# Float32 layers on one core: the parts of p as an interleaved or scattered moving operand, and one gate tile in matmuls of 256 columns

## What is computed

```python
def hybrid_layer(h, p_l, pos, w_in, w_out, g_pre, g_post, g_hg, lb_f, lb_b, w_pg, w_pp, g_ple):
    u = rmsnorm(h, g_pre)
    z = u @ w_in                                   # (512, 2048) @ (2048, 9216)
    ...
    y_hg = o_hg * jax.nn.silu(hg.astype(f32))
    ...
    gate = jax.nn.sigmoid((h @ w_pg).astype(f32))
    e = (p_l @ w_pp).astype(f32)                   # (512, 256) @ (256, 2048)
    h = h + rmsnorm((gate * e).astype(h.dtype), g_ple)
    return h
```

## Time and profile before

| | |
|---|---|
| median of three runs | 3124.75 us |
| span of the profiled execution, first to last instruction | 3121.8 us |
| TensorE matmuls busy | 3041.7 us, 97% |
| TensorE weight loads busy | 2410.3 us, 77% |
| VectorE, ScalarE, GpSimd busy | 53%, 39%, 42% |
| mean granted TensorE clock | 0.992 |

### The profile page before, as it was taken

How to read it: one execution, slowest core, us unless ns; L and a number is a source line. 1 busy time by engine, 2 the same in 40 slices (tenths; PEclk the granted TensorE clock), 3 DMA queues, 4 the chain that set the end, 5 groups by cost and what they waited for, 6 DMA issues and landing times.

```text
span 3121.8 us, 44761 instructions
## 1 busy us (share of the span) xinstructions
PE 3041.7 (97%) x15518; PEld 2410.3 (77%) x15518; DVE 1641.8 (53%) x2261; ACT 1227.8 (39%) x2164; POOL 1316.8 (42%) x1006
## 2 busy tenths in 40 slices
PE   8999999999999999999999999999999999999997
PEld 6877778777777787777777777788777777777886
DVE  5377666554554414657565664461275646645412
ACT  6445444333334333444233333453332333334532
POOL 4444344333334244452434344444534434443444
PEclk9999999999999999999999999999999999999998
DMA  6222212222222323233322222233342222222322
GB/s 240 103 84 98 81 69 82 79 73 76 74 74 81 122 94 135 95 109 121 128 71 97 76 81 84 79 114 129 108 160 90 85 88 81 85 81 81 145 98 94
DMA packets 60872, 307.70 MB, mean 99 GB/s; under 512 B 5712, under 2 KB 6096, under 8 KB 29520
## 3 DMA queue, kind: packets, MB, share of 16 engines
q1 hardware_dynamic: 38224, 259.54, 23.2%
q10 hardware_dynamic: 22528, 46.60, 4.3%
HBM read 287.77 MB, written 18.35 MB: 98 GB/s over the span
## 4 chain that ended last, share of the span: by engine, by line
PE 48%; issue 27%; POOL 14%; DVE 7%; DVEq 2%; ACT 1%; POOLq 0%; DMA 0%; ACTq 0%; SPq 0%
PE z L302 37%; POOL w_low L239 13%; DVE work L1428 2%; DVEq L1510 1%; DVE work L1417 1%; PE z L318 1%; PE turned L302 1%; PE scores L526 1%; PE scores L499 1%; PE o_bank L506 1%; DVE work L1579 1%; PE scores L302 1%; PE scores L536 1%; PE o_bank L546 1%; PE v_bank L335 1%
## 5 line engine op out<-in xcount | busy, mean ns | idle before, releaser
L239 POOL TENSOR_TENSOR w_low<-w_raw,w_high 128x512 fp32r<-128x512 f32 x932 | 1256.0, 1352 | 1785.0 <-ACT w_high L688 1778.3
L302 PE MATMUL z<-u_high,w_high 128*128 128x512 f32 x3408 | 1371.7, 402 | 2.9 <-POOL w_low L239 2.2
L302 PE MATMUL z<-u_high,w_low 128*128 128x512 f32 x3408 | 1329.0, 390 | 0.0
L302 PE MATMUL z<-u_low,w_high 128*128 128x512 f32 x3408 | 1327.7, 390 | 0.0
L688 ACT ACTIVATE w_high<-w_raw 128x512 fp32r<-128x512 f32 x928 | 578.5, 629 | 1275.1 <-PE z L302 1177.4
L302 PEld LDWEIGHTS z<-u_high,w_high 128*128 128x128 f32 x3408 | 640.1, 188 | 149.2 <-issue 16.9
L302 PEld LDWEIGHTS z<-u_low,w_high 128*128 128x128 f32 x3408 | 640.3, 188 | 143.7 <-issue 14.4
L302 PEld LDWEIGHTS z<-u_high,w_low 128*128 128x128 f32 x3408 | 639.6, 188 | 136.1
L1579 DVE TENSOR_TENSOR work<-work 128x512 f32<-128x512 f32 x87 | 99.7, 1146 | 363.8 <-ACT work L935 350.6
L1241 DVE TENSOR_TENSOR work<-z,work 128x512 f32<-128x512 f32 x110 | 76.1, 692 | 166.1 <-PE z L302 145.1
L1269 DVE SCALAR_TENSOR_TENSOR work<-z,work 128x512 f32<-128x512 f32 x56 | 38.7, 692 | 188.9 <-PE z L302 188.3
(11 more groups left out here) (265 smaller groups left out, 3106.9 us busy)
## 6 DMA issues: line engine op xcount, KB each, us to landing
w_raw<-in_wt SPq DMA_DIRECT2D x241, 1024.0 KB, 4.8
out_hT<-work ACTq DMA_DIRECT2D x8, 1024.0 KB, 7.6
work<-out_hT ACTq DMA_DIRECT2D x8, 1024.0 KB, 10.3
work<-in_xT SPq DMA_DIRECT2D x4, 1024.0 KB, 17.9
e_scratch<-work ACTq DMA_DIRECT2D x1, 4096.0 KB, 19.5
work<-in_xT ACTq DMA_DIRECT2D x4, 1024.0 KB, 10.5
work<-in_gw ACTq DMA_DIRECT2D x2, 1792.0 KB, 10.0
work<-in_dec ACTq DMA_DIRECT2D x12, 256.0 KB, 2.6
```

Of the source, the lines that this page charges most:

```text
L239: pool.tensor_tensor(WL[:, 4 * q:4 * q + 4, :], RAW[:, t.odd, 512 * q:512 * q + 512].rearrange("p (k c) -> p k c", k=4), WH[:, 4 * q:4 * q ...
L302: mm = pe.matmul(bank[:], w[:, k, :], u[:, k, :], start=(k == 0 and n == 0), stop=(k == KT - 1 and n == 2))
```

## The change

It has two parts. First, the parts of p are laid out differently in the same four rows of u_low. For k = 0 the high and the low part lie interleaved in rows 12 and 13: element t of the high part at 2t, of the low part at 2t + 1. For k = 1 each part has a row of its own, in another order: token 4a + b lies at 128b + a, so four consecutive tokens are 128 elements apart. The writers (ScalarE's copy and VectorE's subtraction) write in that order, and the matmuls read in token order, so that the bank's columns come out as before. Second, the matmuls of the second gate tile are issued in two halves of 256 columns each, every one with its weight load. `skip_group_check` is a flag of the program's checks and gives no instruction.

```diff
+WHOLE = (slice(0, 512),)
+HALVES = (slice(0, 256), slice(256, 512))
...
-        PH, PL = UL[:, 12:14, :], UL[:, 14:16, :]
+        both = UL[:, 12:14, :].rearrange("p a t -> p (a t)").rearrange("p (t a) -> p t a", a=2)
+        spread = [UL[:, r, :].rearrange("p (b a) -> p a b", b=4) for r in (14, 15)]
+        PH, PL = [both[:, :, 0], spread[0]], [both[:, :, 1], spread[1]]
+
+        def p_order(k, ap):
+
+            return ap.rearrange("p (a b) -> p a b", b=4) if k else ap
...
+            def gate_quarter(t, q, order, gen=None, spare=None, behind=2):
...
+                    for n, (w, u) in enumerate(((WH, UH), (WH, UL), (WL, UH))):
+                        for c in order:
+                            mm = pe.matmul(bank[:, c], w[:, k, :], u[:, k, c], start=(k == 0 and n == 0 and c is order[0]),
+                                           stop=(k == KT - 1 and n == 2), skip_group_check=len(order) > 1)
+                mm.then_inc(sem("w_free"), 1)
...
-                        mm = pe.matmul(Z[m % 2][:], w[:, 2 * n + k, :], u[:, k, :], start=(k == 0 and i == 0),
+                        mm = pe.matmul(p_order(k, Z[m % 2][:]), w[:, 2 * n + k, :], u[k], start=(k == 0 and i == 0),
                                        stop=(k == 1 and i == 2))
...
-                    quarter(Tile(T_HGG + m), q, 0 if m == 0 else None, SPARE.get(m), 4 if m in (4, 5) else 2)
+                    gate_quarter(Tile(T_HGG + m), q, HALVES if m == 1 else WHOLE, 0 if m == 0 else None, SPARE.get(m),
+                                 4 if m in (4, 5) else 2)
...
             for k in range(2):
-                copy(PH[:, k, :], MIX[:, 14 + k, :], "ph_ready")
+                copy(PH[k], p_order(k, MIX[:, 14 + k, :]), "ph_ready")
...
             for k in range(2):
                 v.wait_ge(sem("ph_ready"), k + 1)
-                v.tensor_tensor(PL[:, k, :], MIX[:, 14 + k, :], PH[:, k, :].bitcast(F32),
+                v.tensor_tensor(PL[k], p_order(k, MIX[:, 14 + k, :]), PH[k].bitcast(F32),
                                 ALU.subtract).then_inc(sem("p_split"), 1)
```

More of the change, by code:

```diff
@@ L303, in quarter @@
                                        stop=(k == KT - 1 and n == 2))
+                mm.then_inc(sem("w_free"), 1)
+            def gate_quarter(t, q, order, gen=None, spare=None, behind=2):
+                bank = Z[t.odd] if spare is None else spare
+                if q == 0 and spare is None:
+                    if t.c in (T_HGG, T_HGG + 1):
+                        pe.wait_ge(sem("e_out"), 16)
+                    else:
+                        pe.wait_ge(sem("z_free"), t.times(1, 1 - T_HGG - behind))
+                pe.wait_ge(sem("l_ready"), t.times(4, q + 1))
+                for k in range(4 * q, 4 * q + 4):
+                    if gen is not None:
+                        pe.wait_ge(sem("u_ready"), gen * 16 + k + 1)
+                    for n, (w, u) in enumerate(((WH, UH), (WH, UL), (WL, UH))):
+                        for c in order:
+                            mm = pe.matmul(bank[:, c], w[:, k, :], u[:, k, c], start=(k == 0 and n == 0 and c is order[0]),
+                                           stop=(k == KT - 1 and n == 2), skip_group_check=len(order) > 1)
                 mm.then_inc(sem("w_free"), 1)
```

## The result

The changed kernel takes 3133.77 us (median of five runs, 3133.41 to 3134.44) where the kernel before takes 3124.11 in the runs beside it (five runs, 3123.7 to 3125.0): ratio 1.0032, 95% interval 1.002 to 1.0044, so 9.66 us slower. The forecast was +6.4; the sign was right, the size was not, and the time lies just above the range. The profiled execution took 3133.56 us with a span of 3131.8, 10.0 more than before.

The account below looks back on a forecast made before the run. TensorE's matmuls, filling 97% of the span, were taken as the bound, with slack at two places. Longer reads 9.6 less 3.3 swallowed, +0.1 start, +0 halves gave +6.4 on 3124.75: 3131.2 us, range 3124.3 to 3133.5.

Parts of the forecast that it names:

- Part 1: p's product, 48 matmuls of k = 0 reading every second element: 0 us extra, half rate kept as a rival.
- rival C: p's product: k = 0 at half rate as well as k = 1, +15.9 us, 3140.7 us; chance 0.09.
- Part 2: p's product, scattered reads of k = 1: half rate, +0.213 us for each of 45 matmuls, 9.6 us.
- Part 3: p's product: TensorE's stalls behind late x and weight transfers vanish, swallowing 3.3 of 9.6 us and leaving +6.3 us.
- Part 4: Start of p's product: ScalarE's scattered write of k = 1 delays TensorE by +0.1 us, bounds 0 and +0.6.
- Part 5: Second gate tile as 96 half-width matmuls: -0.3 to +0.6 us, hidden by the third tile's 1.6 us stall, so 0.
- B: p's product: scattered reads are hidden, steps stay 0.227 us, only ScalarE's later start remains, 3124.9 us; chance 0.26.
- A: The forecast itself, p's product: k = 1 at half rate, k = 0 free, 3130.5 to 3132.5 us; chance 0.50.

Follow-up runs that it names:

- The third set of patterns: Kernel before, with chosen read patterns (repeats, alignments) in the 16 banks of p's product and second gate tile in varied widths; steps 0.216 to 0.459 us, no whole time given.

## Why the prediction was wrong, and where it was right

**Part 1, "I take 0 and keep half rate as a rival": the step that failed.** The interleaved read cost 0.220 us a matmul, 9.9 us in all. Row and rule both misled me. VectorE's every second element for nothing says nothing about TensorE's moving operand, for VectorE takes 1.3 ns for each of them (0.679 us / 512) where TensorE takes 0.44 (0.2267 us / 512); I had called it the nearest row and used it as if it were near. And the Trainium skill (Advanced Engine Details and Errata, SBUF Cachelines) asks for two hits on a 16-byte line: I counted an element as a hit, so that every second element had two. The third set of patterns shows that for this stream a hit is an access of two elements. Counted so, the rule holds in all the patterns of the table and gives k = 0 its half rate. It would still have been wrong on k = 1, which has one access on a line at a time and would be at half rate too, as in rival C.

**Part 2, half rate for k = 1, +0.213 a matmul: mis-sized.** It measured +0.057, or +0.045 alone. The sum has a slip as well: it takes the 0.427 against 0.213, though the kernel's own step is 0.2267, and 0.200 x 45 would be 9.0 instead of 9.6. The upper half of the range was never near. The reason given, that the surplus of a steady step shows a stream at the limit of its read rate, was half right: the surplus does belong to the read, for it is gone with two in turn, but an order that is not contiguous can read better, so "scattered" by itself has no price.

**Part 3, 3.3 us of stalls swallowed: right.** 3.4 were, and both waits were gone. (The copy that I put at 22.9 us was done by 22.18, when TensorE restarted; that only widens the margin.) The check on ScalarE held as well: 2.19 us a bank on TensorE left its 3.3 us for two banks as cover.

**Part 4, +0.1 at the start: mis-sized,** 0.82. ScalarE's two copies took 0.49 longer, within the bound of +0.6, but the weight copy behind them starts 0.43 later, and that is only half of the 0.82. The other 0.4 is GpSimd's: its first subtraction ran beside VectorE's scattered one, and the first matmul came 1.86 us behind GpSimd's start where it was 1.48 before. The same distance is 1.87 with only k = 1 scattered (8.60 to 10.47) and 1.86 with only the writes (8.58 to 10.44), and 1.49 with only k = 0 interleaved (8.16 to 9.65). That the two slow each other is the likely reading; no run takes one of them away alone. What the late start is worth depends on the rest: 0 to half a microsecond alone, all of it here.

**Part 5, the tile of halves at 0: right, with its cover.** The tile took 11.5 us, the upper end that was worked out for a surplus for each matmul, and the third tile's stall went from 1.60 to 0.94. The first tile in halves showed the other side: not covered. The Trainium skill (TensorE: Matmul & The Clock Gate, Back-to-back issue gap) gives 2.5 ns over the columns' own time. The trace agrees for the read two in turn at 512 columns (0.216 us) and not for the contiguous one (0.227 us, and 0.118 at 256 columns).

**The rivals.** None was the case. C had k = 0 at half rate, but as an addition to k = 1; B was right about k = 1, for with 0.272 to 0.283 it stays under B's own point of 0.30, and the kernel with that part alone ran within 0.2%. The missing rival was the swap: k = 0 pays and k = 1 doesn't, 45 x 0.213 - 3.3 as in A, with the 2.6 of k = 1 and the 0.8 of the start on top. That A came so near in time is chance: k = 0 was forecast 9.9 us too low and k = 1 7.0 too high, the start 0.7 too low and the swallowed part 0.1 too small, and 6.4 + 9.9 - 7.0 + 0.7 - 0.1 is the 9.9 by which the first gate tile moved. The constant shift from the first gate tile to the end was forecast and came.

## What to carry to other kernels

Price an access pattern on the engine that reads it; another engine's row is no bound. For TensorE's float32r moving operand count accesses of two successive elements in a row on a 16-byte line: one is half rate (every second element 0.451 us, unaligned runs of four 0.452), two is the contiguous read (0.227), four (two places in turn, 0.216) is 5% faster than contiguous, and worth having throughout if the writers can still write contiguously. For orders that come back to a line after others (four in turn, 0.283) this count gives no price: measure them. Look behind each longer step for the next stall that it can use up: the same late start cost at most about 0.5 us in one kernel and 0.8 in another.

## What the hardware showed that I had not expected

- A contiguous float32r row of 512 columns is not the fastest operand: 0.227 us a matmul, and 0.216 with two places in turn, 4, 128, 256, 258 or 512 elements apart.
- Distance adds next to nothing once the rate is halved: every 2nd, 3rd and 4th element 0.451, 0.450, 0.460.
- Alignment alone doubles a step: runs of four every eight elements 0.232 on a line, 0.452 across two.
- ScalarE's copy of 512 elements into float32r takes 0.62 us plain, 1.15 in the mean when it writes two places in turn, and 0.65 to 0.93 when it reads every second element.
- At the start of the program a step is 0.425 us for plain rows, 0.427 for scattered and 0.453 for interleaved ones, while the granted clock of the stretch reads 1.00; there the slower reads are nearly hidden.
